# Head pairs on halves of TensorE's array in a streaming encoder layer

## The reference

```python
# mixer A: 8 heads of 64, own chunk and 8 chunks back (band), relative bias
logits = einsum('bnqhd,bnkhd->bnhqk', q, k) * HEAD_DIM ** -0.5
p = softmax(where(valid, logits + bias, NEG));  oa = einsum('bnhqk,bnkhd->bnqhd', p, v)
# mixer B: an indexer picks 256 keys of each query, then 8 heads on 2 key/value heads
idx = relu(einsum('bthd,bsd->bths', qi, ki))            # 8 index heads of 64
score = einsum('bth,bths->bts', wi, idx);  _, sel = top_k(score, 256)
logits = einsum('btngd,btsnd->btngs', qg, ks) * HEAD_DIM ** -0.5 + t5 bias
p = softmax(logits);  ob = einsum('btngs,btsnd->btngd', p, vs)
y = concatenate([oa, ob]) @ w_out                        # then norms, residual, SwiGLU
```

## Time and profile before

| | us |
|---|---|
| median of three runs | 1935.65 |
| lowest, highest | 1931.89, 1937.73 |
| span of the profiled execution (first to last instruction) | 1930.9 |
| PE busy | 1774.0 (92%) |
| PE weight loads busy | 1436.4 (74%) |
| DVE busy | 819.3 (42%) |
| ACT busy | 651.9 (34%) |
| POOL busy | 139.4 (7%) |

### The profile page before, as it was taken

One profiled execution on the slowest core, in us unless ns is written; L12 is line 12 of the kernel. 1 busy time (PEld: TensorE's weight loads), 2 busy tenths in 40 slices (PEclk: granted clock), 3 DMA queues, 4 the chain that ended last, 5 costly groups with the idle time before them and its releaser, 6 DMA issues. The chain is left out here.

```text
span 1930.9 us, 24858 instructions
## 1 busy us (share of the span) xinstructions
PE 1774.0 (92%) x9641; PEld 1436.4 (74%) x9641; DVE 819.3 (42%) x1606; ACT 651.9 (34%) x1188; POOL 139.4 (7%) x273
## 2 busy tenths in 40 slices
PE   7989799999889988899999399999999998999994
PEld 1145499994357865566654299999999998999994
DVE  0120166668899985455433411111111112444446
ACT  1010145545699953233322411111111111333332
POOL 1100000005211011111101100000000000000000
PEclk9999899999899979989999699999999998999997
DMA  9944531113000030000000311111111113200005
GB/s 344 302 80 50 157 77 44 45 35 110 1 1 1 2 134 22 22 22 23 23 23 25 114 56 43 43 44 54 43 43 43 45 42 148 92 0 0 0 0 204
DMA packets 98951, 123.44 MB, mean 64 GB/s; under 512 B 11402, under 2 KB 70866, under 8 KB 98838
## 3 DMA queue, kind: packets, MB, share of 16 engines
q1 hardware_dynamic: 96892, 116.88, 19.8%
q0 software_dynamic: 1984, 5.57, 0.9%
HBM read 105.44 MB, written 18.96 MB: 64 GB/s over the span
## 5 line engine op out<-in xcount | busy, mean ns | idle before, releaser
L1309 PE MATMUL ps<-h_hi,gu_hi 128*128 128x352 f32 x1056 | 341.7, 324 | 8.0 <-DVE gu_lo L1345 8.0
L1309 PE MATMUL ps<-h_lo,gu_hi 128*128 128x352 f32 x1056 | 339.3, 321 | 0.0
L1309 PE MATMUL ps<-h_hi,gu_lo 128*128 128x352 f32 x1056 | 338.9, 321 | 0.0
L918 PE MATMUL ps<-arena 128*128 128x512 f32 (+5 forms) x464 | 181.3, 508 | 35.6 <-DVE small L1110 18.2
L1309 PEld LDWEIGHTS ps<-h_hi,gu_hi 128*128 128x128 f32 x1056 | 198.8, 188 | 8.1 <-DVE gu_lo L1345 8.1
L1309 PEld LDWEIGHTS ps<-h_lo,gu_hi 128*128 128x128 f32 x1056 | 199.1, 189 | 0.0
L1309 PEld LDWEIGHTS ps<-h_hi,gu_lo 128*128 128x128 f32 x1056 | 198.5, 188 | 0.0
L1398 PE MATMUL ps<-a_hi,wd_hi 128*128 128x352 f32 x528 | 174.1, 330 | 13.9 <-DVE a_lo L1421 13.9
L905 PE MATMUL ps<-arena 128*128 128x64 f32 (+2 forms) x1280 | 165.8, 267 | 7.6 <-DVE arena L976 3.2
L1398 PE MATMUL ps<-a_lo,wd_hi 128*128 128x352 f32 x528 | 171.9, 326 | 0.0
L1398 PE MATMUL ps<-a_hi,wd_lo 128*128 128x352 f32 x528 | 171.4, 325 | 0.0
(11 more groups left out here) (172 smaller groups left out, 2611.7 us busy)
## 6 DMA issues: line engine op xcount, KB each, us to landing
arena<-in_w_ada SPq DMA_DIRECT2D x12, 2048.0 KB, 14.0
gate_raw<-in_w_gate SPq DMA_DIRECT2D x22, 512.0 KB, 3.6
up_raw<-in_w_up SPq DMA_DIRECT2D x22, 512.0 KB, 3.7
arena<-in_w_in SPq DMA_DIRECT2D x16, 512.0 KB, 3.5
hidden<-scratch_y SPq DMA_DIRECT2D x4, 2048.0 KB, 12.2
w_down_all<-in_w_down SPq DMA_DIRECT2D x3, 2560.0 KB, 23.6
arena<-in_x_prompt SPq DMA_DIRECT2D x4, 1024.0 KB, 16.1
arena<-in_w_out SPq DMA_DIRECT2D x2, 2048.0 KB, 10.9
```

The source lines that it names most:

```text
L918: mm = nc.tensor.matmul(ps_cols(B, s_col(s) + lo, hi - lo, r), q, key_source(t, h, lo, hi), start=True, stop=True)
L1309: mm = nc.tensor.matmul(B(3 * i + c, CH), cut[i][a][:, P * k:P * k + P], h[:, NTOK * k + CH * c:NTOK * k + CH * (c + 1)], start=(k == 0 an ...
```

## The change

Heads go in pairs. The pads and POOL's copies are gone: `half_rows` gives the 64 partitions of one head, and the scores of the two heads of a pair are two matmuls, one on rows 0 to 63 of the array and one on rows 64 to 127, into different banks. In the value sums the value block (up to 128 keys x 64) is the stationary operand and the turned P moves; the first head of the pair takes columns 0 to 63, the second 64 to 127, so the sums come out turned and need no O. The reciprocals of the row sums are spread by POOL over 512 columns (L1155 after), turned by four transposes (item R), copied by ACT, and multiplied in by DVE. `pair_plan` gives the order, one pair a step: T items hold two blocks of both heads, each followed by a P item (value sums), W stands in steps 4t+8 and 4t+9. A pair's scores wait for both masks of the pair before; in B's sample tile, where one head needs three banks, the second head's scores wait for the first's mask. A third of the T items is copied by DVE, the rest by ACT. `select` for tile 2 moves into B, and each other one tile later, two parts a step. The projected values and keys are stored apart (NAT and NAR), which frees room.

```diff
-def ring_plan(width, lag, lag_ot, lag_w):
-
-
-
-    units = [(t, h) for t in range(NT) for h in range(HEADS)]
-    last = len(units) + 24
-    plan = []
-    for s in range(last):
+PAIRS = HEADS // 2
+
+
+def pair_plan(width, lag, pv_lag, outproj):
+
+
+
+    pairs = [(t, j) for t in range(NT) for j in range(PAIRS)]
+    steps = len(pairs) + lag + (8 if outproj else 2)
+    plan, pending = [], []
+    for s in range(steps):
         items = []
         u = s - lag
-        if 0 <= u < len(units):
-            blocks = -(-width(units[u][0]) // P)
-            items += [("T", u, b, min(4, blocks - b)) for b in range(0, blocks, 4)]
+        if 0 <= u < len(pairs):
+            blocks = -(-width(pairs[u][0]) // P)
+            for b in range(0, blocks, 2):
+                items.append(("T", u, b, min(2, blocks - b)))
+                pending.append(items[-1])
+                if len(pending) > pv_lag:
+                    items.append(("P", *pending.pop(0)[1:]))
+            if u % PAIRS == PAIRS - 1:
+                items.append(("R", u // PAIRS))
+        elif pending:
+            items += [("P", *it[1:]) for it in pending]
+            pending = []
         for t in range(NT):
-            if s == 8 * t + 8 + lag_ot:
-                items.append(("O", t))
-            if lag_w and s in (8 * t + 8 + lag_w, 8 * t + 9 + lag_w):
-                items.append(("W", t, s - (8 * t + 8 + lag_w)))
+            if outproj and s in (4 * t + 8, 4 * t + 9):
+                items.append(("W", t, s - (4 * t + 8)))
         plan.append(items)
-    return units, plan
+    assert not pending
+    return pairs, plan
...
-def pad_slot(pad, u):
-
-
-    return pad + 256 * (u % 2) + P * (u // 2 % 2)
-
-
-def clear_pads(nc, pool, T, pad, ready):
-    nc.gpsimd.memset(T(pad, 256, HD, HD), 0.0).then_inc(ready, 1)
-    pool.wait_ge(ready, 1)
-    nc.gpsimd.memset(T(pad + 256, 256, HD, 0), 0.0).then_inc(ready, 1)
-    pool.wait_ge(ready, 2)
-
-
-def fill_pad(nc, pool, T, pad, u, q_at, t, h, used, ready):
-
-    if u >= 4:
-        pool.wait_ge(used, u - 3)
-    p0, r = HD * (h % 2), rows_of(t)
-    nc.gpsimd.tensor_copy(T(pad_slot(pad, u), r, HD, p0), T(q_at + NTOK * (h // 2) + P * t, r, HD, p0)).then_inc(ready, 1)
+def half_rows(T, off, n, h):
+
+    return T(off, n, HD, HD * (h % 2))
...
-            for u, (t, h) in enumerate(units):
-                r = rows_of(t)
-                if u >= 2:
-                    pe.wait_ge(relu_done, u - 1)
-                pe.wait_ge(pad_ready, u + 3)
-                q = T(pad_slot(pad, u), r)
+            for p, (t, j) in enumerate(pairs):
+                r = rows_of(t)
+                if p >= 2:
+                    pe.wait_ge(relu_done, 2 * p if t == SAMPLE else 2 * p - 2)
                 for lo, hi in pieces(0, width_b(t), 512):
-                    k = T((KI if t < SAMPLE else KIC if lo < PAST else KI + SEQ - PAST) + lo, hi - lo)
-                    mm = nc.tensor.matmul(B(bank(u), hi - lo, r, c0=lo), q, k, start=True, stop=True)
-                mm.then_inc(idx_mm, 1)
+                    at = (KI if t < SAMPLE else KIC if lo < PAST else KI + SEQ - PAST) + lo
+                    for i in range(2):
+                        mm = nc.tensor.matmul(ps_cols(B, col(p, i) + lo, hi - lo, r),
+                                              half_rows(T, QI + NTOK * j + P * t, r, i),
+                                              half_rows(T, at, hi - lo, i), start=True, stop=True)
+                        if hi == width_b(t):
+                            mm.then_inc(idx_mm, 1)
...
-    LAG, PV_LAG, RING = (3 if band else 2), 2, 3
-    units, plan = ring_plan(width, LAG, LAG + 3, 0 if band else 7)
-    NU = len(units)
+    LAG, PV_LAG, RING = 2, 2, 3
+    pairs, plan = pair_plan(width, LAG, PV_LAG, not band)
+    NP = len(pairs)
     steps = len(plan)
     qk_mm, masked, exp_done = sem(f"qk_mm_{n}"), sem(f"masked_{n}"), sem(f"exp_{n}")
     ring_mm, ring_act, ring_dve = sem(f"ring_mm_{n}"), sem(f"ring_act_{n}"), sem(f"ring_dve_{n}")
-    pv_mm, rinv_done, o_read = sem(f"pv_mm_{n}"), sem(f"rinv_{n}"), sem(f"o_read_{n}")
+    pv_mm, rinv_done, o_read, spread = sem(f"pv_mm_{n}"), sem(f"rinv_{n}"), sem(f"o_read_{n}"), sem(f"spread_{n}")
     pts = [KI, KI + 512, KIC, KIC + 512]
-    pbuf = [QI + 640 * i for i in range(4)] if band else [QI + NTOK * i for i in range(4)]
+    pbuf = [QI + 640 * i for i in range(6)] if band else [QI + NTOK * i for i in range(4)] + [NAT, NAT + NTOK]
     NBUF = len(pbuf)
+    rbn = SCR[1] if band else NAT + 2 * NTOK
...
+    by_dve = [it[0] == "W" and it[2] == 1 or it[0] == "T" and t_seq[it[1:]] % 3 == 2 for it in ring]
...
+    def s_col(t, i):
+        return 0 if in_turn(t) else 1024 * i
...
+                    t, j = pairs[s]
                     r = rows_of(t)
-                    if s >= 2:
-                        pe.wait_ge(masked, s if (t == SAMPLE and not band) else s - 1)
-                    pe.wait_ge(pad_ready, s + 3)
-                    q = T(pad_slot(pad, s), r)
-                    for lo, hi in pieces(0, width(t), 512):
-                        mm = nc.tensor.matmul(ps_cols(B, s_col(s) + lo, hi - lo, r), q, key_source(t, h, lo, hi),
-                                              start=True, stop=True)
-                    mm.then_inc(qk_mm, 1)
-                for j, it in enumerate(plan[s]):
-                    q = first[s] + j
+                    if s:
+                        pe.wait_ge(masked, 2 * s)
+                    for heads in (((0,), (1,)) if in_turn(t) else ((0, 1),)):
+                        if heads == (1,):
+                            pe.wait_ge(masked, 2 * s + 1)
+                        for lo, hi in pieces(0, width(t), 512):
+                            for i in heads:
+                                mm = nc.tensor.matmul(ps_cols(B, s_col(t, i) + lo, hi - lo, r),
+                                                      half_rows(T, q_at + NTOK * j + P * t, r, i),
+                                                      key_source(t, 2 * j + i, lo, hi), start=True, stop=True)
+                                if hi == width(t):
+                                    mm.then_inc(qk_mm, 1)
+                for it in plan[s]:
+                    if it[0] == "P":
+                        _, u, b0, nb = it
+                        t, j = pairs[u]
+                        r = rows_of(t)
+                        ring_read(pe, number[("T", *it[1:])])
+                        if b0 == 0 and j == 0 and t >= 1:
+                            pe.wait_ge(o_read, t)
+                        blocks = -(-width(t) // P)
+                        for i in range(nb):
+                            b = b0 + i
+                            k = block_rows(t, b)
+                            for e in range(2):
+                                mm = nc.tensor.matmul(B(7, r, HD, HD * e, P * j), value_source(t, 2 * j + e, b),
+                                                      T(pts[t_seq[it[1:]] % 4] + P * (2 * i + e), r, k),
+                                                      start=(b == 0), stop=(b == blocks - 1))
+                        mm.then_inc(pv_mm, 1)
+                        continue
+                    q = number[it]
                     bank = 4 + q % RING
                     if q >= RING:
                         ring_read(pe, q - RING)
                     if it[0] == "T":
                         _, u, b0, nb = it
-                        t, h = units[u]
-                        r = rows_of(t)
-                        pe.wait_ge(exp_done, u + 1)
+                        r = rows_of(pairs[u][0])
+                        pe.wait_ge(exp_done, 2 * u + 2)
                         for i in range(nb):
-                            k = block_rows(t, b0 + i)
-                            mm = nc.tensor.transpose(B(bank, r, k, c0=P * i), T(pbuf[u % NBUF] + P * (b0 + i), k, r), ident[0:r, 0:r])
-                        mm.then_inc(ring_mm, 1)
-                        pending.append(q)
-                        if len(pending) > PV_LAG:
-                            pv(pending.pop(0))
-                    elif it[0] == "O":
+                            k = block_rows(pairs[u][0], b0 + i)
+                            for e in range(2):
+                                mm = nc.tensor.transpose(B(bank, r, k, c0=P * (2 * i + e)),
+                                                         T(pbuf[(2 * u + e) % NBUF] + P * (b0 + i), k, r), ident[0:r, 0:r])
+                    elif it[0] == "R":
                         t = it[1]
                         r = rows_of(t)
-                        pe.wait_ge(o_read, t + 1)
-                        for c in range(4):
-                            mm = nc.tensor.transpose(B(bank, r, c0=P * c), T(ONAT + P * c, P, r), ident[0:r, 0:r])
-                        mm.then_inc(ring_mm, 1)
+                        pe.wait_ge(spread, t + 1)
+                        for j in range(PAIRS):
```

(24 more changed lines are left out.)

302 lines of the change are left out of this document (139 added, 163 removed).

## The result

The forecast was 1914 us with a range of 1880 to 1952. The changed kernel took 1969.68 us (median of four runs, 1969.3 to 1976.35) against 1933.77 for the kernel before on the same chip (1930.34 to 1937.73): a ratio of 1.0189, 95% interval 1.0161 to 1.0216. It is slower, by 36 us, and outside the range. The profiled execution has a span of 1968.0 us (before 1930.9).

The account below looks back on a forecast made before the run. TensorE was taken to bound mixer B, three engines together A, mostly VectorE the indexer. From 1930.9, B's 17 and A's 5 came off, giving 1909; adding 4.75 (median above span) gave 1914 us, range 1880 to 1952.

Parts of the forecast that it names:

- rival without overlap: Mixers A and B: packed halves never run side by side, so the kernel takes 1960 us; chance 0.13.
- step 1: Scores on row halves, values on column halves, partly overlapping: saves 44 us in B, 36 in A.
- the rule of order: TensorE in A and B: a pass starts no earlier than the one before; 5 pass times for 8, 3 for 4.
- rival of full overlap: Both heads' passes run side by side in A and B, a shape change costs 0.07 us: 1885 us; chance 0.14.
- step 2: TensorE's array shape changes cost 0.13 us each: 35 us in B (a third later taken as hidden), 27 in A.
- 4 with 5: Mixer B's VectorE queue after the output projection (+16 us), plus smaller items such as sample-tile mask waits and the sums' spread.
- VectorE's queue: Mixer B: the variance read holds back masks; tiles 2 to 6 lose 25 us, less 9 of today's gaps: +16.
- spread: POOL's copy of the reciprocals before item R delays TensorE; 1 us taken, half seen: +4 us over nine tiles.
- the sample's turns: B's sample tile: second head's scores wait 1.7 us for the first's mask, four times: +7 us.
- the bisection's 0.3 a pair: Mixer A: two bisection parts share a step, so waiting for ScalarE's counts costs about 0.3 us a pair.
- A: nothing: Mixer A: a pair stays at 5.3 to 5.4 us against 5.4, since VectorE and ScalarE keep their 5.0.
- The indexer (0): Indexer: -3 us for prompt tiles and pads, +3 for sample pairs waiting for both relus; zero net.

Follow-up runs that it names:

- the four waits: Changed kernel with variance and item R each a step later, bisection parts apart, and the sample tile's second-head scores behind four items: 1911.7 us.
- the grouping: Items ordered T T P P instead of T P T P, against the changed kernel with the four waits removed: 1904.89 us.
- value order: Changed kernel with each value item's passes ordered both blocks of the first head, then both of the second: 1969.68 us, ratio 1.0179 to before.
- the turns: B's sample tile, second head's scores after four items, against the changed kernel with variance and R later and bisection apart: 1911.7 us.

## Why the prediction was wrong

The runs split the change into three parts. From the kernel before, 1933.5, the new form without packing and without the waits, but grouped, costs +39.4 (1972.96); packing gives -68.1 (1904.89); the four waits and the ungrouped items cost +64.8, of which 58.0 the waits and 6.8 the grouping (1969.68). These are differences of medians in a chain, so they add up to the result by construction.

The prediction can be split the same way. Its rival without overlap stood at 1960, so packing was to give -46. The waits that it named make +27. What is left, 1933, is the form alone: -3 against its 1935.65. Against that the runs show:

| part | forecast | measured |
|---|---|---|
| form, ungrouped (39.4 + 6.8) | -3 | +46 |
| packing | -46 | -68 |
| waits in the queues | +27 | +58 |
| sum | -22 | +36 |

So two terms failed, the form by 49 us and the waits by 31, and packing gave back 22 of it by being better than forecast. That the miss was 58 us (56 by the absolute times, as the kernel before came out 2 us lower here) and not 80 is luck. The grouping's 6.8 was measured with packing on; I take it as the same without.

1. **Packing (step 1) was right in kind and too small.** I took 5 passes for 8 and 3 for 4. The runs show half, for scores and values: the rule of order behind my value is false (value order). In the whole kernel it gives 68 where I counted 46. I kept A's 36 almost wholly hidden; A did show 25 of it (212.2 against 187.3) once the form cost something there. The rival of full overlap had the mechanism right. Its time, 1885, was not reached, since it shared all the other steps.
2. **The change of shape (step 2)** measured 0.15 on the timeline and 0.11 to 0.14 by the grouping in B; forecast 0.13. Its size was right.
3. **The failed step that the runs settle best is 4 with 5: what a wait in a queue costs.** I named the four waits at the right places. Forecast: VectorE's queue +16, spread +4, the sample's turns +7, and the bisection's 0.3 a pair netted to 0, in sum 27. Measured by taking them away: 24.8, 19.2 and 6.4 each alone (42.6 together), and 15.4 on top of these; in sum 58.0. Three causes:
   - The clock. "Low clocks go with such gaps; I keep their cost" failed. From the changed kernel to the one with the four waits removed, the stretch of A and B up to the last mask goes from 538 to 483 us. TensorE's idle time is 34 of these 55 us, and 21 are its busy time for the same work, with the granted clock up from 0.80 to 0.83 in A and from 0.85 to 0.91 in B. A lighter TensorE that idles between pairs falls to the lower level in places where the busy one before stayed at full: in A these are windows before (first) and after (second) of 640 keys a tile:

```profile
626.00:670.00 44.00, 44.00 (x312) 36.09 (x313) 40.41 (x143) 41.32 (x84) 4.21 (x16) 1.00 0.00 1
```

```profile
594.00:640.00 46.00, 39.50 (x310) 24.71 (x306) 39.18 (x125) 39.75 (x81) 1.23 (x2) 0.90 0.00 1
```

   - Places left out. R waits in both mixers, 8.3 us in A and 8.5 in B, up to 2.8 at a time. I counted half of one POOL copy a tile, in B alone.
   - The variance's net of 16 was too small, and its gross of 25 meets the measured 24.8 by luck: in the windows above, idle time is only 11 of the 20 us.
4. **The form alone is the larger failure, and it is settled only in part.** I had its changes of shape in the sum (23 us in B after the third that I took off, 0.9 a pair in A), and set the pads, the transposes of O and slack against them. In the profiled execution without packing, A is 25.7 us longer than before, B up to its last mask 3.3, and what follows 11.0. The windows of A and of B to the last mask show where, in the kernel before (first two) and in the one with neither packed:

```profile
516.00:703.00 187.00, 169.50 (x1103) 130.15 (x1104) 166.76 (x594) 165.50 (x370) 21.55 (x77) 0.93 0.01 2
703.00:1030.00 327.00, 305.82 (x1497) 198.55 (x1496) 171.08 (x351) 113.20 (x248) 53.40 (x90) 0.93 0.11 41
517.00:730.00 213.00, 194.87 (x1103) 136.10 (x1101) 164.95 (x579) 164.02 (x356) 5.51 (x9) 0.86 0.01 2
730.00:1059.00 329.00, 319.51 (x1426) 188.81 (x1426) 161.19 (x333) 108.06 (x240) 32.31 (x27) 0.93 0.11 39
```

   In A TensorE is busy 25.4 us longer and idle as before (18); in B it is busy 13.7 longer and idle 12 less, about what the pads' waits were (10.9). By the order of the work there are 110 more changes of shape in A (150 against 40) and 127 in B (180 against 53); at the 0.12 measured by the grouping these are, as an estimate, 13 and 15 us. That is all of B's extra busy time and half of A's; A's other half goes with a granted clock of 0.86 instead of 0.93. The 11 us behind the last mask stay open.
5. **"A: nothing" (5.3 to 5.4 us a pair)** holds for the grouped kernel without the waits (187.3 against 186.5), not for the changed one (200.8). The reason I gave for A, that VectorE and ScalarE keep their 5.0 a pair, is right; what I missed is R's wait (5.7 us in A) and the size of that for the two bisection parts back to back (6.6). Both edits together bring A to 188.3.
6. **The indexer (0)** came out at +1.5, read with the projections ahead of it (518.5 against 517.0); that is within the scatter of this column.
7. **The sample tile and the end.** +7 forecast, +30 measured. 13.6 of it went with the turns (972.9 to 959.3). About 15 us remain in the grouped kernel (957.3 against 942.3), and there the scores of the sample still show

```profile
985.28 3.73 PE L891 MATMUL ps<-arena 64*32 64x512 f32 x6
```

   that is, the lower level. With the turns gone it is not a wait for the mask that brings it. I did not settle what does.

Of the signs that the prediction named, TensorE idle after each W and a longer sample tile came true; A within 180 to 186 and B's gain within 0 to 35 did not (203 by the windows, and 19 longer). The kernel's chance was there: the same packing with five small moves in the order of the queues is 1.5% faster than before (1.2% without the grouping), not 1.9% slower.
